# Norms of a two-block kernel summed in four groups of 32 rows, and output projections placed among the last heads of the attention

## The reference

```python
def rms_norm(x, g):
    return x * lax.rsqrt(jnp.mean(x * x, axis=-1, keepdims=True) + EPS) * g

# first block, layers 0 (latent attention) and 1 (attention with forget gates)
hn = rms_norm(h, norm_pre[i])
proj = hn @ w_in                      # layer 0: c_q and c_kv are normed once more
main = causal attention of 12 heads over 512 tokens, 64 wide
mem_out = attention of 4 heads over 256 memory tokens, 64 wide
y = concat([main, mem_out]) * silu(gate)
h = h + rms_norm(y @ w_out[i], norm_post[i])

# second block, layers 0 and 1, each:
x = x + g_m * mixer(modulate(x, ...))       # modulate: rmsnorm, scale, shift
x = x + g_f * conv_glu_ffn(modulate(x, ...))
return rmsnorm(x, final_g)
```

## Time and profile before

| | us |
|---|---|
| median of three executions | 2110.77 (2104.03 to 2117.55) |
| profiled execution, device time | 2111.71 |
| profiled execution, span | 2110.0 |
| PE busy | 2023.9 (96%) |
| PEld busy | 1566.5 (74%) |
| DVE busy | 1034.8 (49%) |
| ACT busy | 779.4 (37%) |
| POOL busy | 785.4 (37%) |

### The profile page before, as it was taken

The page is one execution under the profiler, slowest core; times in us unless marked ns, Lnnn a source line. Parts: engine busy times, 40 slices in busy tenths (PEclk is TensorE's granted clock), DMA queues, the critical chain, the costliest instruction groups (busy, mean ns, idle before and its releaser), DMA issues.

```text
span 2110.0 us, 23456 instructions
## 1 busy us (share of the span) xinstructions
PE 2023.9 (96%) x9724; PEld 1566.5 (74%) x9724; DVE 1034.8 (49%) x1504; ACT 779.4 (37%) x1187; POOL 785.4 (37%) x333
## 2 busy tenths in 40 slices
PE   6999999899999999998899999999999999999998
PEld 5666666598856589976678888885976777888886
DVE  5332575654465767934575745666501352221324
ACT  4332563423365442155232322324356433222331
POOL 2333463144364253122234344343423324434342
PEclk9999999999999999999999999999999999999999
DMA  5313202255510333121424354342311122223221
GB/s 183 93 57 82 80 1 69 64 162 178 183 37 21 120 125 115 61 80 41 155 84 159 121 189 134 122 141 81 99 60 40 41 80 90 95 89 106 93 73 55
DMA packets 202730, 203.57 MB, mean 96 GB/s; under 512 B 11871, under 2 KB 199523, under 8 KB 202624
## 3 DMA queue, kind: packets, MB, share of 16 engines
q1 hardware_dynamic: 200953, 200.90, 30.0%
q0 software_dynamic: 656, 1.01, 0.3%
q10 hardware_dynamic: 1015, 0.16, 0.1%
HBM read 199.10 MB, written 2.10 MB: 95 GB/s over the span
## 4 chain that ended last, share of the span: by engine, by line
PE 72%; DVE 12%; ACT 6%; POOL 6%; issue 2%; DMA 1%; ACTq 0%; SPq 0%; DVEq 0%
PE bank L507 42%; PE bank L987 15%; POOL wl L2065 6%; ACT wh L1199 3%; PE bank L689 2%; DVE var L1614 2%; PE bank L713 1%; PE bank L810 1%; DVE conv L1960 1%; PE bank L738 1%; DVE conv L1962 1%; PE bank L1056 1%; PE bank L1046 1%; DVE conv L1958 1%; PE bank L534 1%
## 5 line engine op out<-in xcount | busy, mean ns | idle before, releaser
L2065 POOL TENSOR_TENSOR wl<-ring,wh 128x2048 fp32r<-128x2048 f32 (+3 forms) x150 | 645.0, 4301 | 1023.5 <-ACT wh L1199 1023.5
L1199 ACT ACTIVATE wh<-ring 128x2048 fp32r<-128x2048 f32 (+3 forms) x150 | 265.2, 1769 | 239.9 <-PE bank L987 133.0
L507 PE MATMUL bank<-xfh,wh 128*128 128x512 f32 x704 | 276.8, 393 | 10.1 <-POOL wl L2065 7.1
L1582 DVE SCALAR_TENSOR_TENSOR acc<-ring,cs,acc 128x256 f32<-128x256 f32 x336 | 273.3, 813 | 12.0
L507 PE MATMUL bank<-xfh,wl 128*128 128x512 f32 x704 | 274.2, 390 | 0.0
L507 PE MATMUL bank<-xfl,wh 128*128 128x512 f32 x704 | 274.1, 389 | 0.0
L507 PEld LDWEIGHTS bank<-xfh,wh 128*128 128x128 f32 x704 | 132.1, 188 | 45.2 <-POOL wl L2065 11.7
L507 PEld LDWEIGHTS bank<-xfh,wl 128*128 128x128 f32 x704 | 132.2, 188 | 27.7
L507 PEld LDWEIGHTS bank<-xfl,wh 128*128 128x128 f32 x704 | 132.2, 188 | 26.4
L987 PE MATMUL bank<-hsph,wh 128*128 128x512 f32 x352 | 137.8, 391 | 0.0
L987 PE MATMUL bank<-hspl,wh 128*128 128x512 f32 x352 | 137.0, 389 | 0.0
(11 more groups left out here) (391 smaller groups left out, 4254.9 us busy)
## 6 DMA issues: line engine op xcount, KB each, us to landing
ring<-in_ada_w SPq DMA_DIRECT2D x48, 1024.0 KB, 5.3
ring<-in_ffn_w_in SPq DMA_DIRECT2D x44, 1024.0 KB, 5.2
ring<-in_w_in_b SPq DMA_DIRECT2D x14, 1024.0 KB, 5.4
ring<-in_even_w_in SPq DMA_DIRECT2D x14, 1024.0 KB, 5.1
ring<-in_ffn_w_out SPq DMA_DIRECT2D x16, 768.0 KB, 4.4
ring<-in_odd_w_in SPq DMA_DIRECT2D x12, 1024.0 KB, 5.3
ring<-in_ffn_w_out SPq DMA_DIRECT2D x16, 640.0 KB, 4.3
ring<-in_w_out SPq DMA_DIRECT2D x8, 1024.0 KB, 5.3
```

Of the source, the lines that this page charges most:

```text
L507: mm = eng.matmul(o, l_, r_, start=(first and i == 0), stop=(last and i == 2))
L1199: eng.activation(wh[:, m % SPLIT, 0:w], ring[:, n % RING, 0:w], ACT.Copy).then_inc(wh_ready, 1)
L1582: ins = eng.scalar_tensor_tensor(out=s, in0=w[:, k, :], scalar=cs[:, k:k + 1], in1=s, op0=ALU.mult, op1=ALU.add)
L2065: eng.tensor_tensor(wl[:, m % SPLIT, 0:w], ring[:, n % RING, 0:w], wh[:, m % SPLIT, 0:w].bitcast(F32), ALU.subtract).then_inc(wl_ready, 1)
```

## The change

1. Norms. The sum of squares of tokens 128g to 128g+127 goes to partitions 32g to 32g+31 (`group_sums`: four matmuls with 32 columns of ones, 128 tokens each), so that `var` is 128x128, of which there are two now. `inverse` and `root` work on 128x128. Then PE spreads the root over a bank again (`norm_spread`: four float32 matmuls of 128 columns with a column of the identity, broadcast), and DVE reads the 128x512 factor from that bank of the rotation.
2. The norms of `c_q` and `c_kv` follow each other at once, both sums first, then both roots and both spreads.
3. `load_roots` makes ACT take one root of a single column before the norm needs it: at the start, after sine and cosine, and at the start of `out_first` and of `out_second`.
4. The matmuls of `warm` around the norms are fewer: 2 and 3 around a spread where there were 7, and one between the sums of the pre-norm.
5. In the attention ACT and DVE split gated tiles 0, 1 and 2 in steps 13, 14 and 15 and tiles 3 to 6 in step 16. PE puts the first two chunks of the output projection between the transposes and applications of the last heads.

```diff
+EARLY = {13: (0,), 14: (1,), 15: (2,), 16: (3, 4, 5, 6)}
...
-        var = sb("var", [P, S])
+        var = sb("var", [P, 2, P])
...
+            def group_sums(src, groups, first, last):
+                for g in groups:
+                    mm = eng.matmul(ssq_bank[g * GROUP:(g + 1) * GROUP, 0:P], ones[:, 0:GROUP], src[:, g * P:(g + 1) * P],
+                                    start=first, stop=last, skip_group_check=True)
+                return mm
+            def norm_spread(last_use, groups=NB):
+                k = counts["spread"]
+                b = bank(("rs", k), last_use)
+                pe.wait_ge(rstd_ready, k + 1)
+                rows = groups * GROUP
+                for g in range(groups):
+                    pick = ident[0:rows, g * GROUP:g * GROUP + 1].to_broadcast([rows, P])
+                    mm = eng.matmul(b[:, g * P:(g + 1) * P], pick, var[0:rows, k % 2, :], start=(g == 0), stop=(g == groups - 1),
+                                    skip_group_check=True)
...
+            for k in range(2):
+                ssq(k, KT)
+            norm_spread((mem_normed, KT), 2)
+            for k in range(2, KT):
                 ssq(k, KT)
...
             for t in range(3):
                 ssq(t, 3)
-            warm(5)
             for t in range(2):
                 ssq(t, 2)
+            warm(1)
+            norm_spread((cq_normed, 3))
+            norm_spread((cq_normed, 5))
...
+                for h in range(16):
+                    scores(h)
                     if h >= 3:
                         apply((h - 3) // 2, (h - 3) % 2)
                     if h == 1:
                         warm((6, 9)[l], aside=True)
-                    if 1 <= h <= 16:
+                    if h >= 1:
                         transposes(h - 1)
+                apply(6, 1)
+                first = chunk(stage)
+                outputs(0, *first, range(2), range(5))
+                transposes(15)
+                outputs(0, *first, range(2), range(5, 7))
+                apply(7, 0)
+                apply(7, 1)
+                second = chunk(stage)
+                outputs(1, *second, range(1), range(6))
+                outputs(0, *first, range(2), range(7, KT))
+                chunk_done(first[0])
+                ada_sums(1)
+                outputs(1, *second, range(1), range(6, KT))
+                outputs(1, *second, range(1, 2), range(KT))
+                chunk_done(second[0])
...
-                for c in range(4):
+                for c in range(2, 4):
...
                 ssq_summed()
-                warm(7)
+                warm(2)
+                norm_spread((post_scaled, KT * (l + 1)))
+                warm(1)
                 for t in range(KT):
                     ssq(t, KT)
-                warm(7)
+                    warm(int(t < KT - 1))
+                warm(2)
+                norm_spread((scaled, KT * (l + 2)))
+                warm(3)
...
                 if last:
                     ssq_summed()
-                    warm(7)
+                    warm(2)
+                    norm_spread(last)
+                    warm(3)
...
+            def load_roots():
+                chain.link(eng.activation(early[:, :], ones[:, 0:1], ACT.Sqrt))
...
             eng.activation(cos[ropes, :], cos[ropes, :], ACT.Sin).then_inc(sin_ready, 1)
+            load_roots()
...
-                    if h >= 1:
+                    if 1 <= h < 16:
+                        transposed(eng, act, l, h - 1, "act")
+                    for t in EARLY.get(h, ()):
+                        wait_emptied(act, ("o", l, t))
+                        high(gate[:, t, :], ys[0][:, t, :])
+                    if h == 16:
                         transposed(eng, act, l, h - 1, "act")
...
             def out_second(*stage):
+                load_roots()
...
+            inverse(3, Q_LORA)
+            inverse(2, KV_LORA)
+            scale_by(2, cq, cq, [vec("q_norm_a", t) for t in range(3)], cq_normed)
+            scale_by(3, ckv, ckv, [vec("kv_norm_a", t) for t in range(2)], cq_normed)
             lows(cq, cqs, 3)
-            normed(2, KV_LORA, ckv, ckv, [vec("kv_norm_a", t) for t in range(2)], cq_normed)
             lows(ckv, ckvs, 2)
...
+                    for t in EARLY.get(h, ()):
+                        low(gate[:, t, :], (ys[0][:, t, :], ys[1][:, t, :]))
```

More of the change, by code:

```diff
@@ L444, in warm @@
                 elif len(rotation) >= ROT:
-                    _, who, nth, _ = tiles[rotation[-ROT]]
-                    pe.wait_ge(emptied[who], nth + 1)
+                    free(rotation[-ROT])
                 b = ssq_bank if aside else banks[len(rotation) % ROT]
@@ L533, in ssq @@
                     counts["hn"] += 1
-                eng.matmul(ssq_bank[:, :], ones, sq[:, i % 2, :], start=(t == 0), stop=(t == total - 1)
-                           ).then_inc(sq_used, 1)
+                group_sums(sq[:, i % 2, :], range(NB), t == 0, t == total - 1).then_inc(sq_used, 1)
                 counts["sq"] += 1
@@ L544, in ssq_summed @@
                 pe.wait_ge(sq_added, counts["sq_sum"])
-                eng.matmul(ssq_bank[:, :], ones, sq_sum[:, :], start=True, stop=False).then_inc(sq_used, 1)
+                group_sums(sq_sum, range(NB), True, False).then_inc(sq_used, 1)
                 for t in (KT - 2, KT - 1):
@@ L967, in _, with out_second @@
             warm(4)
-            def out_second(stage, parts, xs, ready, last=True):
+            def out_second(stage, parts, xs, ready, last):
                 for c in range(4):
@@ L1016, in ffn @@
                         ada_sums(0)
-                    out_second((f"ffn{l}.out", part), 2, hsp, f"ffn{l}/{part}", last=(part == 1))
+                    out_second((f"ffn{l}.out", part), 2, hsp, f"ffn{l}/{part}",
+                               ((scaled, 5 * KT), (out_normed, KT))[l] if part else None)
             ffn(0)
@@ L1248, in _ @@
                 if k == 1:
-                    root(M)
+                    root(2 * GROUP)
             for t in range(KT):
@@ L1325, in out_first @@
                 stage = ("out_a", "out_b")[l]
-                for t in range(KT):
-                    wait_emptied(act, ("o", l, t))
-                    high(gate[:, t, :], ys[0][:, t, :])
+                wait_emptied(act, ("o", l, KT - 1))
+                high(gate[:, KT - 1, :], ys[0][:, KT - 1, :])
+                load_roots()
                 for t in range(KT):
@@ L1602, in add_squares, with inverse @@
                 used["squares"] += 2
-            def inverse(count, width, n=S, squares=None):
+            def inverse(count, width, groups=NB, squares=None):
                 k = used["norm"]
@@ L1761, in out_first @@
             def out_first(l):
-                lows(gate, ys, KT)
+                low(gate[:, KT - 1, :], (ys[0][:, KT - 1, :], ys[1][:, KT - 1, :]))
                 for pair in range(3):
```

106 lines of the change are left out of this document (71 added, 35 removed).

## The result

The changed kernel takes 2099.41 us in the median (2094.21 to 2101.53), the kernel before 2110.01 (2104.03 to 2117.55), each over nine executions; the ratio is 0.9947 with a 95% interval of 0.9935 to 0.9959. The forecast was 2087.7 with a range of 2079 to 2098, so less than half of the 23.1 us came. The profiled execution of the changed kernel is its fastest, 2094.21. I therefore read a second one as well, of the same kernel in a later comparison (*again*: median 2096.07, profiled execution 2097.15, span 2095.0).

The account below looks back on a forecast made before the run. PE's weight matmuls hold over half the chain; the change shortens links between. Opening 1.4, latent norms 6.3, drains 4.0, layer norms 4.4, other norms 1.6, 1.6, 1.3, 2.5 sum to 23.1: 2110.8 - 23.1 = 2087.7 us, range 2079 to 2098.

Parts of the forecast that it names:

- The price of a norm: From last square to first scaling a norm takes 3.5 us instead of 6.0, a gain of 2.5 at the scaling.
- the latent norms: Grouped norms of c_q and c_kv let the gate's second chunk start at 147.6 instead of 153.86: gain 6.3 us.
- The norms of the layers: Post- and pre-norms gain 1.5 us each, 6.0 over two layers, less 1.6 for the clock: +4.4.
- Bounds 0 and 3 for each post-norm; I take 0.8: PE's idle 3.7 us behind a post-norm may bring a stretch at 1.2 GHz; charged -1.6 in all.
- The early table loads: ACT's early root costs 1.5 us behind the cosine, and 0.3 at the norm behind `odd_out`.
- The opening: Scaling of `mem` isn't held by POOL: 2.9 us earlier, less 1.5 for the root behind the cosine: +1.4.
- The drains: Early projection chunks at the attentions' last heads gain 3.6 and 0.4 us, +4.0, bounds 6.6 and -1.8.
- nothing waits for POOL: Upper bound at the attentions' ends: low parts run at once beside POOL's scalings, gain 6.6 us.
- the drain gives nothing: Rival: attention low parts wait to the end of POOL's three instructions; 2094, or 2096 with the low clock; chance 0.20.
- The gain is larger: Rival: POOL doesn't hold the low parts and the residual add; gain 32 us, 2079; chance 0.10.
- The gain of opening and latent norms is given back: Rival: PE arrives earlier and waits for weights; 7.7 us lost, gain 15, 2095; chance 0.07.
- The slower rival: With fewer fillers the clock falls in every norm, 3 us for each of eleven; 2121; chance 0.05.

Follow-up runs that it names:

- late_roots: Changed kernel with the later projections' early root-table load moved behind the third tile's weight split, and dropped in ffn's first parts; 2095.35 us, ratio 0.9932.
- drain_only: Kernel before with only the changed kernel's end of the attentions, no grouped norm and no early table; 2104.47 us, ratio 0.9978.
- norms_only: Changed kernel with the attentions' end as before: no early split, four projection chunks behind the last head; 2102.69 us, ratio 0.9966.
- half_fill: Changed kernel with the filler between the pre-norms' sums half as wide (256 columns); 2090.92 us, ratio 0.9916.
- tuned_latent: Changed kernel with late table load, five fillers behind post-norm spreads, half-width fillers between sums, and a filler ahead of the latent sums; 2087.39 us, ratio 0.9888.
- best: As tuned_latent, plus no root behind the cosine, x's spread ahead of mem's first chunk, and SBUF addresses as before; 2084.96 us, ratio 0.9884.
- same_place: Changed kernel with the early root's tile widened to 256 columns, so later SBUF tiles keep their earlier addresses; 2095.36 us, ratio 0.993.
- no_cos_root: Changed kernel without the early root and its table load behind the cosine; 2094.68 us, ratio 0.994.

## Why the prediction was wrong

**The price of a norm was right.** Reciprocal 0.95, root 0.31; behind `even_out` the scaling came 2.6 earlier (2.5), the first tile of ffn0 1.6 earlier (1.6), since the low part took 1.97 and ended 0.6 behind POOL's `wl`. The norm behind `odd_out` won 1.6 (1.3; the 0.3 that I charged it was lost too, but ahead of it, in `odd_out`), the last one 2.6 (2.5), the latent norms 6.3 in the first profile (6.3). In the second they won 5.1, because the clock fell inside them.

**The norms of the layers failed: "Now PE needs 0.43 + 0.88 for each".** The filler between two sums takes 1.05, not 0.88, which I had from seven in a row. With the sum's 0.36 that is 1.41 for a tile, above DVE's 1.20 and above my 1.31, so the fillers themselves made the path: 0.7 us in seven tiles beyond my sum, in each of two layers. With the clock at 2.4 GHz that is all that is missing: 3.0 - 0.7 = 2.3 was forecast so, and 2.2 to 2.3 was won. Then the clock. "Bounds 0 and 3 for each post-norm; I take 0.8": measured by filling the gap, it was 1.4 and 2.4, most of it by way of the fillers, which are longer at 1.2 GHz. Together 0.7 x 2 + 3.8 - 1.6 = 3.6 of the 3.9 that are missing. Both mechanisms were in the working, both too small.

**The early table loads failed in two places.** I charged the one behind the cosine, rightly (1.53 for 1.5), and 0.3 for that in `odd_out`. ScalarE: Activation LUTs, "What ACT_TABLE_LOAD costs", in the Trainium skill, would have it 1.38 dearer for a drain; the trace doesn't agree, the operation behind the load at 1366.70 starts 0.01 behind its end. The loads in ffn's last parts, for which the sum had nothing, stand ahead of the first weight copy, for which PE waits: 1.6 and 0.8, given back by *late_roots*. I hadn't followed POOL's `wl` and PE behind that copy at the two places where the stage starts.

**The opening was half right.** `mem`'s scaling took 3.2 without a wait (3.3), and PE began its chunk 4.0 earlier (34.5 for 38.6). "Less 0.1 for the spread that PE makes between two chunks" failed: the clock was at 1.2 GHz from 27 to 40 (0.50 over 30 to 35 and 35 to 40 in *again*; before has 3.4 us of it, *drain_only* none, all fourteen traces with grouped norms 10 to 17 from 24 on), the chunk's products came every 0.21 instead of 0.12, and the spread stood behind them. From the end of `x`'s transposes to the last low part of `x`, 1.0 to 1.5 were won instead of 2.9, which the load behind the cosine takes back. The 1.7 in the first profile's table is luck: 1.5 of it is transposes that ended earlier in that execution.

**The drains were under-rated.** They gave 4.8 and 2.1 for 3.6 and 0.4 (0.6 of the 2.1 is won in *norms_only* too, without the drain). Together that is about my bound of 6.6, "nothing waits for POOL", where I had taken a low part that waits for a border of POOL's three scalings. Changed kernel, DVE, then POOL:

```profile
308.24 0.71 DVE L1740 TENSOR_TENSOR ysl<-gate,ysh 128x512 fp32r<-128x512 f32 x1 [0.44 <-ACT ysh L1296]
308.88 0.74 DVE L1852 TENSOR_REDUCE mx<-bank 128x1 f32<-128x256 f32 x2
...
307.17 3.39 POOL L2198 TENSOR_SCALAR probs<-probs,rinv 128x256 f32<-128x256 f32 x3 [1.90 <-DVE rinv L1858]
312.17 3.44 POOL L2198 TENSOR_SCALAR probs<-probs,rinv 128x256 f32<-128x256 f32 x3 [1.60 <-DVE rinv L1858]
317.22 4.30 POOL L2198 TENSOR_SCALAR probs<-probs,rinv 128x256 f32<-128x256 f32 x3 [1.61 <-DVE rinv L1858]
```

The second of POOL's three by itself, changed kernel and before:

```profile
308.24 1.43 POOL L2198 TENSOR_SCALAR probs<-probs,rinv 128x256 f32<-128x256 f32 x1
```

```profile
316.15 0.92 POOL L2084 TENSOR_SCALAR probs<-probs,rinv 128x256 f32<-128x256 f32 x1
```

The low part ran at once, in 0.71, and POOL's second scaling became longer. That doesn't refute the rule by which whoever starts first holds the port (the Trainium skill, SBUF — State Buffer, "Who interferes with whom"): the low part came right at the border. ACT's high part ended 1.31 behind the start of head 13's inverse sums (306.90 to 308.21) and POOL's border lay 1.34 behind it. I had it end at 1.42, by letting it start at the end of ACT's record before it; it starts 0.15 ahead of that end. So an error of 0.1 chose the wrong case. In all fourteen traces with this drain the low parts of steps 13 to 15 start 0.00 to 0.08 behind a border; none comes by itself in the middle of a scaling, so what would happen there isn't shown. (In step 16 two low parts start 0.4 and 1.0 into POOL's third scaling, right behind another low part; they took 0.68 and 0.88 and the scaling 1.82, so there neither waited for the other's end.) At a border it isn't settled either: 0.07 behind POOL's start in step 14 DVE wasn't held, 0.03 behind a `wl` (30.52 and 30.55 in before) it was. Head 14's maxima came 1.2 late (1.9), head 15's inverse sums 1.7 (3.3). PE waited 1.4 for the third chunk's `wl` (1.2).

**What no step had.** The addresses: 1.2 us in ffn0 and 0.9 in ffn1 by POOL's weight operation, which the prediction never touched. And the even stage, 1.6 slower with nothing changed in it: the changed kernel had 0.88 of the clock over 965:1037, before 0.91 over the same work. All of the 1.6 goes in the last 14 us of the stage, where the clock was at 1.2 GHz once more for 3.4 us (from 1025). The other traces agree: nine, both profiles of the changed kernel among them, have such a stretch at this place and lose 1.5 to 3.0 there, the six without it (*half_fill*, *tuned_latent*, *best* and three more) lose at most 0.5. In the mLSTM it is the other way round: before has two stretches of 3.4 us at 1.2 GHz there (1579 and 1630), the changed kernel one (1543), and that is 1.6 of the 2.8 won, luck and not the change. Why the clock falls where it does stays open.

**The rivals.** The one nearest to the result, "the drain gives nothing", 2094 to 2096, has the wrong mechanism: it was the drains that gave all and more. "The gain is larger" was right for the drains alone; `wl` did hold the residual addition and the low part behind `even_out`. "The gain of opening and latent norms is given back" happened in part in *again*, 4.9 instead of 7.7, and not in the first profile, by the clock and the spread's place in PE's queue and not by weights. The slower rival, a clock falling in every norm, was right only behind the two post-norms and, in some executions, in the latent norms.

## What to carry over

Before a wait is shortened, look at what lay beside it: a filler must be shorter than the interval at which the real work arrives, measured alone between two such pieces and not in a row of its own kind, and long enough in sum that PE doesn't idle. An "early" operation is free only if nothing is queued behind it on its engine for which PE waits; follow it in each place where the program issues it. And take a second profile of the changed kernel before accounting for microseconds, because two executions of it differed here by 3 in the first 140 us.

## What I had not expected of the hardware

- POOL's 128x2048 operation took 4745 ns or 4675 ns by the addresses of its tiles alone (*same_place*), and PE felt it in 0.08 steps. Which address matters (the offset of 1024 bytes or of the small tile) wasn't tried, nor why.
- POOL's subtraction held DVE's two-input operation to its end (2.43 for 0.69). Where DVE's low part started within 0.08 of a border between POOL's scalings, it wasn't held, and POOL's scaling became longer, 1.43 for 0.92.
- The same idle stretch behind layer 1's post-norm was followed by 6.8 us at 1.2 GHz in *again* and by none in *norms_only* and *no_cos_root*.
- With a sum and no filler the same norm was faster at a lower clock (0.77 for 0.84 over 22 us, 3.0 us faster). Here the clock was worth something only where PE was what was waited for.
